# Hybrid decoder block: expert weights fetched in pairs of chunks with 16 KB runs

## The reference

```python
def moe_ffn(hn, w_router, b_router, w_gu, b_gu, w_down, b_down):
    logits = (hf @ w_router + b_router)           # hf: 256 x 1024, 32 experts
    top_v, top_i = lax.top_k(logits, TOP_K)       # TOP_K = 4
    gate = jax.nn.softmax(top_v, axis=-1)
...
    def expert_block(args):
        xb, e = args
        gu = xb @ w_gu[e] + b_gu[e]               # w_gu[e]: 1024 x 2048
        g_lin = jnp.minimum(gu[..., :D_FF], SWIGLU_LIMIT)
        u_lin = jnp.clip(gu[..., D_FF:], -SWIGLU_LIMIT, SWIGLU_LIMIT)
        act = g_lin * jax.nn.sigmoid(SWIGLU_ALPHA * g_lin) * (u_lin + 1.0)
        return act @ w_down[e] + b_down[e]        # w_down[e]: 1024 x 1024
```

## Time and profile before

| | |
|---|---|
| median of 3 runs | 1360.6 us (1358.38 to 1360.81) |
| profiled execution: time, span | 1358.64 us, 1356.8 us |
| mean granted TensorE clock | 0.965 of full speed |
| busy: TensorE, VectorE, ScalarE, GpSimd | 1243.8, 333.8, 232.2, 203.4 us |
| moved by DMA | 452.17 MB in 78999 packets |

### The profile page before, as it was taken

One profiled execution on the slowest core, in us unless ns is written; L12 is line 12 of the kernel. 1 busy time (PEld: TensorE's weight loads), 2 busy tenths in 40 slices (PEclk: granted clock), 3 DMA queues, 4 the chain that ended last, 5 costly groups with the idle time before them and its releaser, 6 DMA issues.

```text
span 1356.8 us, 14696 instructions
## 1 busy us (share of the span) xinstructions
PE 1243.8 (92%) x5915; PEld 613.4 (45%) x5915; DVE 333.8 (25%) x452; ACT 232.2 (17%) x292; POOL 203.4 (15%) x82
## 2 busy tenths in 40 slices
PE   5998987998789999999999999999999999999986
PEld 5996765787663333333333333333332333333332
DVE  3825357224341121112111111211211121111113
ACT  3554376243300000001000000100000010000000
POOL 5755544666100000000000000000000000000000
PEclk8899988998969999999999999999999999999998
DMA  8523524443729999999999999999999999999993
GB/s 287 178 91 120 171 93 136 135 154 130 287 116 358 423 421 420 421 421 420 421 421 422 420 421 420 420 421 420 421 421 421 421 420 421 421 421 421 422 420 128
DMA packets 78999, 452.17 MB, mean 333 GB/s; under 512 B 7092, under 2 KB 7256, under 8 KB 29736
## 3 DMA queue, kind: packets, MB, share of 16 engines
q1 hardware_dynamic: 78200, 448.87, 81.8%
q0 software_dynamic: 720, 2.20, 0.6%
HBM read 450.00 MB, written 1.05 MB: 332 GB/s over the span
## 4 chain that ended last, share of the span: by engine, by line
PE 49%; SPq 28%; DMA 12%; issue 4%; DVE 3%; ACT 1%; POOL 1%; DVEq 0%; POOLq 0%; ACTq 0%
SPq L414 20%; PE ps L861 11%; PE ps L560 10%; SPq L419 8%; PE ps L895 7%; PE ps L549 6%; DMA gates<-in_w_gu 6%; DMA ring<-in_w_gu 6%; PE ps L807 3%; PE ps L833 2%; PE ps L841 2%; PE ps L575 1%; PE ps L590 1%; POOL w_lo L357 1%; PE ps L645 1%
## 5 line engine op out<-in xcount | busy, mean ns | idle before, releaser
L357 POOL TENSOR_TENSOR w_lo<-ring,w_hi 128x2048 fp32r<-128x2048 f32 x40 | 187.8, 4699 | 130.0 <-ACT w_hi L941 129.8
L861 PE MATMUL ps<-ring,xs 128*64 128x512 f32 x768 | 177.9, 605 | 16.2 <-DMA ring<-in_w_gu 9.9
L861 PE MATMUL ps<-ring,nT 128*64 128x512 f32 x768 | 176.5, 597 | 16.5 <-DMA ring<-in_w_gu 16.2
L895 PE MATMUL ps<-ring,xbuf 128*64 128x512 f32 x768 | 173.2, 597 | 0.0
L1137 ACT ACTIVATE xbuf<-xbuf 128x512 f32<-128x512 f32 x32 | 20.1, 630 | 795.1 <-DVE xbuf L1534 795.1
L446 POOL TENSOR_SCALAR ss<-ss 128x2 f32<-128x2 f32 (+1 forms) x6 | 1.1, 190 | 1016.4 <-DVE ss L1168 999.6
L1534 DVE TENSOR_SCALAR xbuf<-ps 128x512 f32<-128x512 f32 x32 | 22.1, 692 | 470.6 <-PE ps L861 470.6
L861 PEld LDWEIGHTS ps<-ring,xs 128*64 128x64 f32 x768 | 53.3, 139 | 137.6 <-issue 102.5
L861 PEld LDWEIGHTS ps<-ring,nT 128*64 128x64 f32 x768 | 51.8, 137 | 137.5 <-issue 86.3
L895 PEld LDWEIGHTS ps<-ring,xbuf 128*64 128x64 f32 x768 | 52.2, 137 | 117.4 <-issue 117.4
L1552 DVE COPY xbuf<-ps 128x512 f32<-128x512 f32 x32 | 22.1, 692 | 322.2 <-PE ps L895 322.2
(11 more groups left out here) (291 smaller groups left out, 1323.3 us busy)
## 6 DMA issues: line engine op xcount, KB each, us to landing
ring<-in_w_gu SPq DMA_DIRECT2D x192, 1024.0 KB, 26.3
ring<-in_w_down SPq DMA_DIRECT2D x96, 1024.0 KB, 26.4
ring<-in_w_in SPq DMA_DIRECT2D x24, 1024.0 KB, 5.2
small<-in_w_gu SPq DMA_DIRECT2D x16, 1024.0 KB, 26.5
kv<-in_w_gu SPq DMA_DIRECT2D x16, 1024.0 KB, 26.8
xn<-in_w_gu SPq DMA_DIRECT2D x16, 1024.0 KB, 26.4
gates<-in_w_gu SPq DMA_DIRECT2D x16, 1024.0 KB, 26.0
xn<-in_w_down SPq DMA_DIRECT2D x8, 1024.0 KB, 26.6
```

The lines of the kernel that those rows point to most:

```text
L357: ops.tensor_tensor(w_lo[:, m % SPLIT, :], ring_slot(m), w_hi[:, m % SPLIT, :], ALU.subtract).then_inc(lo_ready[name], 1)
L861: i = mm(ps[64 * half:64 * half + 64, 4 + q, :], xg[:, k, (j % GE) * SLOTS:(j % GE + 1) * SLOTS], w[:, q * FF + half * 512:q * FF + half * ...
L895: i = mm(ps[64 * half:64 * half + 64, 6, :], actT[:, c, fh * 64:fh * 64 + 64], w[:, k % 2, half * 512:(half + 1) * 512], start=(k == 0), s ...
```

## The change

Expert weights are fetched in pairs of chunks, 2 MiB per DMA. The ring has eight pairs of slots (`PAIRS`), each with a semaphore of its own (`pair_full`). A partition now receives 16 KB that lie together in memory: two successive rows of gate/up weights, or four of down weights. `chunk_used` counts pairs in the expert stage, after a pair's second chunk. Row order within a pair is thus 2p + k in place of 128k + p; to match it, `hn2` is written with its columns permuted (`pair_rows`, `paired`), the router's weights and the gain are loaded in the same order (the gain in a tensor of its own, `gmoe`, by GpSimd's queue, no longer through `prow`), and the activation is written with a stride of four. To have pairs side by side, `w_hi` and `w_lo` are interleaved, `kv` and `small`, and half of `gates` and `xn`, lie next to each other, and the first eight fills have a new order (`PAIR_ORDER`).

```diff
-RING_MOE = 16
+PAIRS = 8
+GU_PR = KD // 2
+EXP_PR = GU_PR + FF // P // 4
...
-MOE_ORDER = ([m % RING_SPLIT for m in range(LAST_RAW, FRONT_CH)] + [SMALL_SLOT, KV_SLOT, X_SLOT]
-             + halves_of(FRONT_CH - 3) + [XN_SLOT, GATES_SLOT] + halves_of(FRONT_CH - 2) + halves_of(FRONT_CH - 1))
+def halves_pair(m):
+    return (HALF_SLOT + 2 * (m % SPLIT)) // 2
+KV_SMALL, GATES_XN = RING // 2, RING // 2 + 1
+PAIR_ORDER = [1, X_SLOT // 2, KV_SMALL, halves_pair(FRONT_CH - 3), 0, GATES_XN,
+              halves_pair(FRONT_CH - 2), halves_pair(FRONT_CH - 1)]
+STEP_PR = BODY * EXP_PR
...
+        def pair_rows(t):
+            return t[:].rearrange("p b (c q k) -> p b c k q", q=P, k=2)
+        def paired(t):
+            return t.rearrange("p b (c k q) -> p b c k q", k=2, q=P)
...
+        def pair(m):
+            q = PAIR_ORDER[m % PAIRS]
+            return {KV_SMALL: kv_small, GATES_XN: gates_xn}[q][:, :, :] if q >= RING // 2 else ring[:, 2 * q:2 * q + 2, :]
...
             def first_free(q):
-                if q < RING_SPLIT:
-                    eng, count = lo_count(LAST_RAW + q)
+                if PAIR_ORDER[q] in (0, 1):
+                    eng, count = lo_count(FRONT_CH - 1 if PAIR_ORDER[q] == 0 else LAST_RAW + 1)
                     sp_.wait_ge(lo_ready[eng], count)
...
+            def expert_pairs(it, g, first=False):
                 for j in range(BODY):
-                    for c in range(EXP_CH):
-                        m = FRONT_CH + j * EXP_CH + c
+                    for c in range(EXP_PR):
+                        m = j * EXP_PR + c
...
-                            sp_.wait_ge(chunk_used, it * STEP_CH + (m - RING_MOE + 1))
-                        if c < KD:
-                            src = w_gu[0, bass.ds(g * BODY + j, 1), c * P:(c + 1) * P, :]
-                            sp_.dma_start(ring_slot(m),
-                                          src.rearrange("e p n -> (e p) n")).then_inc(slot_full[slot(m)], 16)
+                            sp_.wait_ge(chunk_used, it * STEP_PR + (FRONT_CH + m - PAIRS + 1))
+                        if c < GU_PR:
+                            src = w_gu[0, bass.ds(g * BODY + j, 1), c * 2 * P:(c + 1) * 2 * P, :]
+                            sp_.dma_start(pair(m), src.rearrange("e (p k) n -> p (e k) n", p=P)
+                                          ).then_inc(pair_full[m % PAIRS], 16)
...
-            pool.dma_start(wr[:], w_router[0].rearrange("(k p) n -> p k n", p=P)).then_inc(late_in, 16)
+            pool.dma_start(wr[:].rearrange("p (c k) n -> p c k n", k=2),
+                           w_router[0].rearrange("(c p k) n -> p c k n", p=P, k=2)).then_inc(late_in, 16)
+            pool.dma_start(gmoe[:].rearrange("p (c k) -> p c k", k=2),
+                           g_moe[0].rearrange("(c p k) -> p c k", p=P, k=2)).then_inc(late_in, 16)
...
                     for k in range(KD):
-                        m = FRONT_CH + j * EXP_CH + k
-                        pe.wait_ge(slot_full[slot(m)], it * (16 * STEP_CH // RING_MOE) + filled(m))
-                        w = ring_slot(m)
+                        m = j * EXP_PR + k // 2
+                        if k % 2 == 0:
+                            pe.wait_ge(pair_full[m % PAIRS], it * (16 * STEP_PR // PAIRS) + pair_filled(m))
+                        w = pair(m)[:, k % 2, :]
...
-                        i.then_inc(chunk_used, 1)
+                        if k % 2:
+                            i.then_inc(chunk_used, 1)
...
-            normalise(hn2, h, 10, 5)
+            normalise(paired(hn2), pair_rows(h), 10, 5)
...
-                    V.tensor_tensor(actv.rearrange("s (i k q) -> s i k q", i=2, k=2),
-                                    ul.rearrange("s (i q k) -> s i k q", i=2, k=2),
-                                    sg.rearrange("s (i q k) -> s i k q", i=2, k=2), ALU.mult).then_inc(act_ready, 1)
+                    V.tensor_tensor(actv.rearrange("s (k q) -> s k q", k=4), ul.rearrange("s (q k) -> s k q", k=4),
+                                    sg.rearrange("s (q k) -> s k q", k=4), ALU.mult).then_inc(act_ready, 1)
```

More of the change, by code:

```diff
@@ L158 @@
 SQUARED = {"x": 1, "y": 5, "mem": 7, "h1": 8, "h2": 9, "final": 10}
[L162 to L163 removed]
+ROW_MIX, ROW_XATTN, ROW_MEM, ROW_SSD = 0, KD, 2 * KD, 3 * KD
+ROW_CW = 4 * KD
 ROW_CB = ROW_CW + CONV * NCB
@@ L310, in build @@
             sem, ("x_in", "prm_in", "dtw_in", "mem_in", "late_in", "moe_in", "gf_in"))
-        slot_full = [sem(f"slot_full{i}") for i in range(RING_MOE)]
+        slot_full = [sem(f"slot_full{i}") for i in range(RING_SPLIT)]
+        pair_full = [sem(f"pair_full{i}") for i in range(PAIRS)]
         chunk_used = sem("chunk_used")
@@ new lines, in expert_pairs @@
+                    for c in range(EXP_PR):
+                        m = j * EXP_PR + c
+                        if first and m < PAIRS:
+                            first_free(m)
+                        else:
+                            sp_.wait_ge(chunk_used, it * STEP_PR + (FRONT_CH + m - PAIRS + 1))
[3 more added lines that the diff above has]
+                                          ).then_inc(pair_full[m % PAIRS], 16)
+                        else:
+                            r = (c - GU_PR) * 4 * P
+                            src = w_down[0, bass.ds(g * BODY + j, 1), r:r + 4 * P, :]
+                            sp_.dma_start(pair(m).rearrange("p a (k n) -> p (a k) n", k=2),
@@ L420, in expert_chunks @@
                                           src.rearrange("e (p k) n -> p (e k) n", p=P)
-                                          ).then_inc(slot_full[slot(m)], 16)
-            expert_chunks(0, 0, first=True)
+                                          ).then_inc(pair_full[m % PAIRS], 16)
+            expert_pairs(0, 0, first=True)
             with sp_.Fori(1, NIT) as g:
-                expert_chunks(g, g)
+                expert_pairs(g, g)
             with sp_.If(overflow_cond(sp_)):
@@ L888, in experts @@
                     for k in range(FF // P):
-                        m = FRONT_CH + j * EXP_CH + KD + k // 2
-                        if k % 2 == 0:
-                            pe.wait_ge(slot_full[slot(m)], it * (16 * STEP_CH // RING_MOE) + filled(m))
-                        w = ring_slot(m).rearrange("p (k n) -> p k n", k=2)
+                        m = j * EXP_PR + GU_PR + k // 4
+                        if k % 4 == 0:
+                            pe.wait_ge(pair_full[m % PAIRS], it * (16 * STEP_PR // PAIRS) + pair_filled(m))
+                        w = pair(m).rearrange("p a (k n) -> p (a k) n", k=2)
                         fh, c = k // 4, k % 4
@@ L1174, in normalise, with take_transposed @@
                 for b in blocks:
-                    V.tensor_scalar(dst[:, b, :], src[:, b, :], ss[:, c0 + b:c0 + b + 1], None,
+                    V.tensor_scalar(dst[:, b], src[:, b], ss[:, c0 + b:c0 + b + 1], None,
                                     ALU.mult).then_inc(normed, 1)
-            def take_transposed(n, dst, row):
+            def take_transposed(n, dst, gain):
                 for half in range(2):
@@ L1184, in take_transposed @@
                         d = dst[:, 4 * half:4 * half + 4, b * P:(b + 1) * P]
-                        g = pcol[:, row + 4 * half:row + 4 * half + 4].unsqueeze(2).broadcast_to([P, 4, P])
+                        g = gain[:, 4 * half:4 * half + 4].unsqueeze(2).broadcast_to([P, 4, P])
                         V.tensor_tensor(d, src, g, ALU.mult).then_inc(tr_out, 1)
```

85 lines of the change are left out of this document (40 added, 45 removed).

## The result

The kernel after takes 1346.95 us (median of 4 runs, 1345.89 to 1349.07), the kernel before 1360.7 us beside it (4 runs, 1358.38 to 1361.03). The ratio is 0.9906, with a 95% interval of 0.9894 to 0.9919: about 13.7 us less. The forecast was 1351.3 us, 9.3 us less; its mechanism held; the saving per pair of chunks was taken somewhat too small, and some 2 us of the difference stay without a term of their own.

What follows compares the result with a forecast made beforehand. Weight transfers by full DMA engines were taken to bound the expert stage. Terms -12.7 + 1.7 + 1.7 = -9.3 us gave 1349.3 against the profiled execution, 1351.3 as median; forecast's own range 1346 to 1357, 8 in 10 1342 to 1362.

Steps and rivals of the forecast that it cites:

- The bound: Expert stage: full DMA engines set the pace, 29.9 us of transfers per expert against 27.2 us of TensorE work.
- Fewer, longer packets: Expert weight stream: 8 packets per engine and one increment fewer save 70 ns per pair, 12.7 us over 182 pairs.
- the rule of about 3 fixed cycles per packet: Skill's estimate for weight packets: 515 cycles in place of 518 for 16 KB, 29 ns per pair, 5.3 us in all.
- The first slot comes back later: Start of the expert stream: TensorE releases a pair after its second chunk, so the restart moves 1.7 us later.
- The dry spell: Stream running short in 430 to 435 us, 1.7 us lost before: no longer than before by more than 0.7 us.
- The last pair is used later: End of the expert stage: two chunks, not one, to multiply after the last gate/up data land, 1.7 us more.
- The permuted columns: VectorE's strided product stays at 0.69 us with a stride of four; up to 1.2 us more would be hidden.
- The norm in the router's stage: Reads h with a stride before the router: ScalarE costs nothing more, VectorE's slowdown up to 1.1 us stays hidden.
- The issue for the gain: g_moe's DMA moved to GpSimd's queue: 0.55 us, covered by GpSimd's 4.39 us wait for ScalarE.
- The full fixed part: Rival on expert weight packets: 14.4 ns fixed per packet, 129 ns saved per pair, 1340.5 us; chance 0.14.
- The run that buys next to nothing: Rival on weight packets: hardware cuts 16 KB in two, or fixed part 3 ns or less; 1362.9 or 1358.5 us; chance 0.18.
- A loss by a stride of 16 KB through memory: Rival in the expert stage: partitions starting 16 KB apart share banks; 1% per pair gives 1373 us; chance 0.12.

Runs made afterwards that it cites:

- the 4 KB kernel: Kernel after with runs of 4 KB, each pair fetched by two DMAs of 1 MiB: 1389.24 us, ratio 1.0215 to before.
- the first experiment: Kernel after with its 2 MiB pairs, but runs of 8 KB and no permuted columns: 1360.53 us, ratio 1.0006 to before.
- the transfers alone: All computation removed, expert weights streamed with runs of 2 to 32 KB and DMAs of 1 to 4 MiB: 422 GB/s at 8 KB, 429 at 16 KB.
- the second experiment: Kernel before with its DMAs kept, but TensorE waits for and releases chunks by twos: 1361.88 us, ratio 1.002 to before.

## Why the prediction was right, and where it was off

The direction, the mechanism and its place held; the time lay 4.4 us below the forecast, inside its own range.

- **The bound.** Transfers set the pace of the expert stage before and after; TensorE's room of 2.7 us per expert let the saving through almost one for one.
- **Fewer, longer packets** is the term of the sum that was mis-sized: 70 ns per pair and 12.7 us were taken, 78 ns and 14.1 us came. The fixed part of a packet was taken as 8 ns, between 4.6 and 14.4 from two pairs of rows. The run sizes measured alone give 9.4 to 9.6 ns at every step from 2 to 32 KB, the 4 KB kernel 9.3, and the step from the first experiment to after 9.3. An increment was taken as 6 ns, and the first experiment shows 3. So the packets account for nearly all of it. The prediction's 4.6 ns came from short stretches and from shares that count more than the whole of an engine's time (101.1%); by the bytes moved in the transfers alone, 4 against 8 KB gives 9.4. That the 8 came near was in part luck, as its bounds left room for half and for twice as much.
- By the rule of about 3 fixed cycles per packet (the Trainium skill, DMA: Bandwidth & Descriptors, "Why small descriptors are slow") 29 ns per pair were to be gained, an estimate; the trace doesn't agree, at 78.
- **The first slot comes back later**: restart at 411 us forecast, 411.1 seen; behind the first gate/up product it is 1.5 us later, against 1.7. **The dry spell** was to be no longer; it cost 0.9 us in place of 1.7.
- **The last pair is used later**: 1.7 forecast, 3.58 - 1.86 = 1.7 seen. The cost of pairs as a whole, 3.4 in the sum, measures 2.7 us (1.5 to 3.9) in the second experiment and 0.8 (-0.4 to 2.0) in the first. The medians of these two kernels with the same waits differ by 1.35 us; their profiles show 1.0 of it, half in the increments and half in the dry spell.
- **The permuted columns.** The prediction expected VectorE's product to stay at 0.69 us with a stride of four elements. That was wrong: it takes 1.08 us. The cover that it named, up to 1.2 us, hid it, as the timeline of after shows for the first expert:

```profile
422.88 1.08 DVE L1568 TENSOR_TENSOR xbuf<-xbuf 128x512 f32<-128x512 f32 x1
```

- The norm in the router's stage, which answers to the earlier trace rows, took 1.25 us on ScalarE (1.15 before) and 0.75 on VectorE (as before): 0.1 us, where nothing was taken.

```profile
371.37 1.25 ACT L972 ACTIVATE gates<-h,ss 128x1024 f32<-128x1024 f32 x1 [1.25 <-POOL ss L469]
371.37 0.75 DVE L1200 TENSOR_SCALAR gates<-h,ss 128x1024 f32<-128x1024 f32 x1 [1.16 <-POOL ss L469]
```

- The issue for the gain takes 0.76 us on GpSimd's queue, and GpSimd then still waits 3.77 us for ScalarE where it waited 4.39. The cover held.
- **The rivals.** The full fixed part, 14.4 ns, falls by the transfers alone, at 9.4 to 9.6. The time lies where the prediction put the half way to this rival, 11 ns and 1347 us; the packets don't bear that out, so this is a coincidence. The run that buys next to nothing falls by the packets of 16 KB and 13.6 us between the first experiment and after. A loss by a stride of 16 KB through memory falls by 429 GB/s at 16 KB and 432 at 32 KB.
- **The sum, made again.** With the measured terms it is -14.1 of packets and increments, 1.5 and 1.7 of the pairs at the two ends and -0.8 of the dry spell: -11.7 us. The ratio's interval says -11.0 to -14.4, so it lies inside, but 2 us from the middle. From the first experiment to after the 13.6 us are those of the run. What is left lies between before and the first experiment: 1.8 us more by these terms (1.5 + 1.7 - 0.6 of increments - 0.8), 0.8 measured, within its interval. The rest is open. The combine's 1.1 us and the front's 0.3, which stand between the two profiles, are of the granted clock and of those executions.

## What to carry to other kernels

When the windows show the DMA engines full, the bytes per packet are what is left to gain. Read the time of a packet at two sizes, from the bytes moved in a long window. Twice the time of the one less the time of one twice as long is the fixed part. Here it is 9 to 10 ns; the rate gains 2.9% from 4 to 8 KB, 1.7% from 8 to 16, 0.7% from 16 to 32. Multiply it by the packets that lie between the stream's start and its last wait. A larger unit gives part of it back at both ends, one unit's work at the first release and one at the last use; splitting only these two units is where to look next, and it pays only as far as no dry spell follows. Keep every DMA on all 128 partitions, or on partitions in steps, and let a permuted column order absorb the row order that a long run brings.

## What the hardware showed that was not expected

A DMA of 1 MiB to 64 neighbouring partitions runs at half the rate, 212 GB/s against 429 for every second partition, with the engines shown full (1.01 in both); two such halves in one queue don't make up for each other, and the kernel went from 1347 us to 2193 in the median and 1907 at best. The Trainium skill (SBUF — State Buffer, "Door 1: The DMA port swizzle") says that the seventh bit of the partition number picks the port of each pair, so that 0 to 63 reach 8 of 16 ports; the 212 and 429 agree with it.

With DMAs of 1 MiB and 8 KB runs the median time from issue to landing was 27.1 us, though 16 MiB were allowed in flight; with 4 MiB and runs of 8 to 32 KB it was 39.1 us. At 422 GB/s, 27.1 us hold about 11 MiB, at 39.1 us all 16:

```profile
ring<-in_w_gu SPq DMA_DIRECT2D x48, 4096.0 KB, 39.1
ring<-in_w_gu SPq DMA_DIRECT2D x64, 1024.0 KB, 27.1
```

So the queue held less than was allowed. No single number fits: with DMAs of 2 MiB the median times in the windows of 2, 4 and 8 KB runs are 19.9, 24.1 and 33.1 us, which at their rates are 235, 151 and 107 packets per engine, against 87 with DMAs of 1 MiB and 8 KB. What the limit is stays open; it cost nothing here, as the engines stayed full.

VectorE's product of two operands of 128x512 costs 0.69 us when it reads every second float32, as much as without a stride in the version with runs of 4 KB, and 1.08 us when it reads every fourth. The Trainium skill (SBUF — State Buffer, "Door 1: The DMA port swizzle") speaks of lines of 16 bytes that want two hits each; a stride of two has them, a stride of four hasn't, and the two durations agree.

Left open: what makes the front's length vary by 3.0 us, what decides how soon the clock falls in the last combine, and why the 16 DMA engines end the stream some 8 us apart in both kernels. After's windows show it as the earlier trace rows did:

```profile
1312.00:1314.00 2.00, 0.89 (x4) 0.34 (x6) 0.00 (x0) 0.00 (x0) 0.00 (x0) 1.00 0.85 360
...
1320.00:1322.00 2.00, 2.00 (x14) 0.97 (x12) 0.79 (x3) 0.94 (x2) 0.00 (x0) 1.00 0.19 82
```
